# A bidirectional state-space scan: decay, step and mask in one array, both directions in one product

## What is computed

```
y[t] = sum over s <= t of exp(c_f[t] - c_f[s]) * (C[t].B[s]) * dt_f[s] * x[s]      forward
     + sum over s >= t of exp(c_b[t] - c_b[s]) * (C[t].B[s]) * dt_b[s] * x[s]      backward
     + what the carried states of other chunks add, for each direction
```

## Time and profile before

| | |
|---|---|
| median of three runs | 3008.32 us (2997.15 to 3011.02) |
| the profiled execution | 3002.91 us |
| its span in the trace | 3001.1 us |
| PE busy | 2875.6 us, 96% of the span |
| DVE, ACT, POOL busy | 846.9, 733.4, 245.7 us |
| granted PE clock, mean | 0.982 |

### The profile page before, as it was taken

How to read it: one execution, slowest core, us unless ns; L and a number is a source line. 1 busy time by engine, 2 the same in 40 slices (tenths; PEclk the granted TensorE clock), 3 DMA queues, 4 the chain that set the end, 5 groups by cost and what they waited for, 6 DMA issues and landing times.

```text
span 3001.1 us, 30849 instructions
## 1 busy us (share of the span) xinstructions
PE 2875.6 (96%) x12370; PEld 1831.9 (61%) x12370; DVE 846.9 (28%) x1568; ACT 733.4 (24%) x1712; POOL 245.7 (8%) x262
## 2 busy tenths in 40 slices
PE   7989998999997999999999999999999799999999
PEld 6768884555544666444444444445666577788888
DVE  1330005455463333200121000006555433202110
ACT  1330012554554333100011000004544422201100
POOL 3000001232331000000000000001212200000000
PEclk8999999999998999999999999999999999999999
DMA  9336765333331121122252442425334222357652
GB/s 230 85 103 174 196 195 144 101 98 96 93 100 42 51 56 50 56 74 76 75 175 81 122 126 77 126 74 149 101 99 110 64 71 71 83 151 214 177 152 87
DMA packets 530157, 330.40 MB, mean 110 GB/s; under 512 B 27504, under 2 KB 496864, under 8 KB 530016
## 3 DMA queue, kind: packets, MB, share of 16 engines
q1 hardware_dynamic: 519184, 296.36, 35.7%
q0 software_dynamic: 10528, 31.46, 4.3%
q10 hardware_dynamic: 304, 0.61, 0.1%
HBM read 327.05 MB, written 1.34 MB: 109 GB/s over the span
## 4 chain that ended last, share of the span: by engine, by line
PE 83%; ACT 7%; DVE 5%; issue 2%; PEld 1%; DMA 1%; DVEq 1%; POOL 0%; PEldq 0%; POOLq 0%; ACTq 0%; SPq 0%
PE ps L956 61%; PE ps L1388 4%; PE ps L1379 4%; PE ps L1370 3%; PE ps L1297 2%; ACT TMP L784 2%; DVE TMP L1841 2%; PE ps L1407 2%; PE ps L982 1%; PE ps L1428 1%; ACT TMP L790 1%; PE ps L966 1%; ACT BIG L796 1%; PEld ps L956 1%; DMA BIG<-bias_lines 1%
## 5 line engine op out<-in xcount | busy, mean ns | idle before, releaser
L956 PE MATMUL ps<-xnT,W 128*128 128x512 f32 (+2 forms) x4064 | 1326.5, 486 | 15.6 <-DVE TMP L1623 7.0
L956 PEld LDWEIGHTS ps<-xnT,W 128*128 128x128 f32 (+1 forms) x4064 | 772.1, 191 | 529.7 <-issue 449.9
L956 PE MATMUL ps<-BIG,W 128*128 128x256 f32 (+1 forms) x2528 | 773.3, 467 | 5.3 <-DVEq L402 2.7
L956 PEld LDWEIGHTS ps<-BIG,W 128*128 128x128 f32 x2528 | 481.1, 191 | 291.1 <-issue 245.9
L1841 DVE SCALAR_TENSOR_TENSOR TMP<-ps,prmT,TMP 128x510 f32<-128x510 f32 (+3 forms) x256 | 182.5, 714 | 141.1 <-ACT TMP L763 125.2
L597 ACT ACTIVATE xnT<-hT 128x512 f32<-128x512 f32 (+1 forms) x48 | 25.1, 523 | 568.0 <-DVE hT L1772 467.1
L574 ACT ACTIVATE TMP<-ps 128x512 f32<-128x512 f32 (+4 forms) x150 | 85.0, 572 | 233.1 <-PE ps L1388 94.3
L1772 DVE SCALAR_TENSOR_TENSOR hT<-ps,modc,hT 128x256 f32<-128x256 f32 x48 | 21.8, 481 | 374.2 <-PE ps L956 374.2
L555 POOL TENSOR_TENSOR BIG<-BIG,TMP 128x512 f32<-128x512 f32 x80 | 107.9, 1364 | 186.6 <-ACT BIG L796 186.6
L1388 PE MATMUL ps<-W,xnT 128*128 128x128 f32 x1024 | 122.6, 276 | 0.0
L2030 DVE TENSOR_TENSOR BIG<-TMP 128x512 f32<-128x512 f32 (+1 forms) x64 | 35.8, 559 | 303.1 <-ACT TMP L926 303.1
(11 more groups left out here) (273 smaller groups left out, 2134.5 us busy)
## 6 DMA issues: line engine op xcount, KB each, us to landing
W<-in_w_in SPq DMA_DIRECT2D x192, 512.0 KB, 4.0
W<-in_w_mlp SPq DMA_DIRECT2D x128, 512.0 KB, 4.1
W<-in_ada_w SPq DMA_DIRECT2D x96, 512.0 KB, 3.8
BIG<-cs_rows POOLq DMA_DIRECT2D x96, 256.0 KB, 4.8
W<-in_w_ssd_o SPq DMA_DIRECT2D x32, 512.0 KB, 4.0
W<-in_w_gate SPq DMA_DIRECT2D x22, 512.0 KB, 5.1
W<-in_w_up SPq DMA_DIRECT2D x22, 512.0 KB, 4.7
W<-in_w_down SPq DMA_DIRECT2D x16, 512.0 KB, 4.2
```

Of the source, the lines that this page charges most:

```text
L956: last = mm(dst, w[:, c, 0:m], rhs(k), start=k == 0, stop=k == total - 1)
```

## The change

The multiplication by the step dt moves from x to the masks, and the masks of the two directions are added before the product. `xc` holds plain x, once instead of twice, written by a copy. `masked` is now eight instructions of 128 columns, each `mt` times the step (a column of one number for each partition, out of `tabs`) times `cbm`, then a drain, then one addition of 512 columns that puts the sum into the first direction's buffer. `mready` counts chunks instead of directions. `outputs` has one term in place of two for the work inside the chunk. The other arrays keep their places in memory: a gap of 1024 columns is left where the second half of `xc` was.

```diff
@@ the arrays
-        (tabs, ssq, xs, xc, xcd, cbm, btm, mt, H, ysq) = carve(
-            TMP, (4, 4, 64), (T,), (4, T), (2, 4, S), (2, 2, S), (2, 4, P), (T,), (4, 4, P), (2, 3, S), (2, T))
+        (tabs, ssq, xs, xc, _, xcd, cbm, btm, mt, H, ysq) = carve(
+            TMP, (4, 4, 64), (T,), (4, T), (4, S), (D,), (2, 2, S), (2, 4, P), (T,), (4, 4, P), (2, 3, S), (2, T))
@@ PE, outputs
-                    R("mready", 2 * (n_ch * g + i) + 2)
+                    R("mready", n_ch * g + i + 1)
...
-                        for d in range(2):
-                            terms.append([(xc[:, d, ch, h * HD:(h + 1) * HD], mt[:, (2 * (n_ch * g + i) + d) % 4, h, :])
-                                          for h in (2 * pair, 2 * pair + 1)])
+                        terms.append([(xc[:, ch, h * HD:(h + 1) * HD], mt[:, (2 * (n_ch * g + i)) % 4, h, :])
+                                      for h in (2 * pair, 2 * pair + 1)])
@@ DVE, masked
                         c = 2 * (n_ch * g + i) + d
                         R("mexp", c + 1)
-                        V.tensor_tensor(mt[:, c % 4, :, :], mt[:, c % 4, :, :],
-                                        cbm[:, d, order[i], :].unsqueeze(1).to_broadcast([P, 4, P]), ALU.mult)\
-                            .then_inc(ssd[l, "mready"], 1)
+                        for h in range(4):
+                            V.scalar_tensor_tensor(out=mt[:, c % 4, h, :], in0=mt[:, c % 4, h, :],
+                                                   scalar=tabs[:, 0, order[i], span(g * 4 + 32 * d + h, 1)],
+                                                   in1=cbm[:, d, order[i], :], op0=ALU.mult, op1=ALU.mult)
+                    dve.drain()
+                    V.tensor_tensor(mt[:, (c - 1) % 4, :, :], mt[:, (c - 1) % 4, :, :], mt[:, c % 4, :, :], ALU.add)\
+                        .then_inc(ssd[l, "mready"], 1)
@@ DVE, xc
-                    for d in range(2):
-                        for b in range(n_ch // 2):
-                            last = V.tensor_tensor(
-                                xc[:, d, 2 * b:2 * b + 2, :].rearrange("p c (h e) -> p c h e", e=HD),
-                                PS[4 + b][:, :].rearrange("p (c h e) -> p c h e", c=2, e=HD),
-                                tabs[:, 0, 2 * b:2 * b + 2, span(g * 4 + 32 * d, 4)].unsqueeze(3)
-                                .to_broadcast([P, 2, 4, HD]), ALU.mult)
+                    for b in range(n_ch // 2):
+                        last = V.tensor_copy(flat(xc[:, 2 * b:2 * b + 2, :]), PS[4 + b][:, :])
```

## The result

The changed kernel takes 3026.86 us, the median of five runs (3023.43 to 3027.55), against 3008.31 us for five runs of the kernel before. The ratio is 1.007, with a 95% interval of 1.0048 to 1.0092: slower by 0.7%. In a later set of runs (experiment 11) the same pair gave 1.0076 (1.0062 to 1.0089). The forecast was +5 us on the profiled execution; its span went from 3001.1 to 3025.1 us, +24.

What follows compares the result with a forecast made beforehand. PE was taken as the bound, busy 96% of the span, except where outputs 1 in layer 0 wait for DVE. Terms 2.0 + 1.6 - 6.4 + 2.0 + 5.8 gave +5 us, on base 3006: 3011 us, range 2999 to 3029.

Steps and rivals of the forecast that it cites:

- The size of a masked: DVE, both scans: eight instructions, drain and addition take 2.93 us, 1.64 more than before (bounds 1.2 and 2.3 more).
- The stop: PE's wait ahead of outputs 1 in layer 0 grows from 1.79 to 3.9 us.
- A group of layer 0 without the clock: Layer 0, groups 0 to 6: masked 1 adds 1.64 us, outputs 1 to 3 lose 0.455 and 0.91; +0.28 a group.
- Layer 1: Layer 1, groups 0 to 6: outputs 0 and 1 lose 0.91 us a group, nothing takes it back; -6.4 us.
- The clock: Layer 0, PE's stop ahead of outputs 1: granted clock falls in half of seven groups, 1.65 us each; +5.8 us.
- The last groups: Last group of each layer, no fronts to cover the longer masks: +1.6 us in layer 0, +2.0 in layer 1.
- The slower one: Rival: layer 0's clock falls in every group and DVE steps do not overlap; +19 us, 3025 us, chance 0.18.

Runs made afterwards that it cites:

- experiment 11: The changed kernel itself, run again beside the kernel before on the same chip: 3022.16 us, ratio 1.0076.
- experiment 1: Changed kernel plus 14 overwritten PE products between outputs 0 and outputs 1, layer 0, groups 0 to 6: 3010.53 us, ratio 1.0029 to the kernel before.
- experiment 5: Changed kernel without the masks' addition, so PE multiplies two terms as before, with the eight masking instructions kept: 3024.69 us, ratio 1.0087 to the kernel before.

## Why the prediction was wrong

It said "no change" with 0.78 and gave "slower" 0.18. By its own steps:

- **The size of a masked, right where POOL is quiet.** A step of 0.26 us and 2.17 us for eight instructions were forecast from the earlier trace rows; 2.18 was measured. The stop was forecast at 3.9 us; it is 3.89 in six groups (2.49 in group 0, which started from 0.38). The rule of the Trainium skill (VectorE: DVE Perf Modes, The DRAIN you can't avoid), weighed there, would have given 2.8 us for the eight. The same section ends by saying that an operation which is not held starts earlier, and the prediction left that out; the trace agrees with the exception: each took 0.347 us at the median and the step was 0.26.
- **A group of layer 0 without the clock, right.** +0.28 forecast, +0.36 in experiment 1.
- **Layer 1, right in the main.** -0.91 a group forecast, -0.85 measured; over the six periods in the table -4.5 where the sum had -5.5, since two of them were 0.4 and 0.2 us longer.
- **The clock, wrong, and the largest miss.** The text had both facts: 1.79 us keeps the clock, 4.3 us loses it, and 3.9 is nearer the latter. It then counted "a fall in half of the seven groups", +5.8 us, because 3.9 was shorter than any stop with a row. The clock fell in all six groups with a stop of that length, for 2.0 us each: 12 us, 6 more than counted (and in all seven in experiment 11). The price of 1.65 us was too low as well, and it was a mean over 15 us in which PE was busy for only 7.3; the full cost is what the products behind the stop take more. Experiment 1 shows the cause by taking it away, experiment 5 that even 2.7 us would have been too long. The Trainium skill (TensorE: Matmul & The Clock Gate, Part 1), which has an idle array fall back to half its rate, was cited beside this step and agrees with the trace; it was given half its weight.
- **The last groups, undersized.** +1.6 and +2.0 us were forecast, +6.7 and +4.5 came (the table's 5.9 and 3.7 begin at front 2 of group 6 and so hold what the outputs of that group gained). Two steps failed. The first priced the products there as if their speed stayed as it was. In layer 0 outputs 1 and the states behind them took 4.0 us at 0.50 instead of 2.6 at 1.00, +1.4 where the sum had -0.5; in layer 1 the outputs took 5.40 us at 0.50 throughout, where before the clock was back at 0.91 in their second half (5.20), +0.2 where the sum had -1.3, and 0.5 us more came behind them. The second put POOL at nothing on DVE: of the +3.9 us up to outputs 1 in layer 0 (+2 forecast) 1.7 are masked 0 and `carried` beside POOL's multiplications. In layer 1 DVE's +3.8 is near the forecast 3.3. The prediction had named this collision only as something that might make masked 2 or 3 late in the middle groups, where it turned out to be covered.
- **The rivals.** The slower one had the right mechanism (the stop ahead of outputs 1 decides by its length) and tied it to steps on DVE that do not overlap. That condition was not needed: the point from which it decides lies near 2.5 us, not at 4.5. Its size, 3025, is right by luck in part: it had 6.6 us for the seven groups where 2.5 came, and 3.5 each for the last ones where 6.7 and 4.5 came.

A slip without effect: the row of outputs 2 and 3 is 64 MATMUL records, two for each of 32 products, and not 32 of them and 32 weight loads; it is 16 terms either way.

Summed by the prediction's own terms:

| term | forecast | from the two chains |
|---|---|---|
| layer 0, groups 0 to 6, without the clock | +2.0 | +2.5 |
| the clock in these groups | +5.8 | +12 |
| layer 0, last group | +1.6 | +6.7 |
| layer 1, groups 0 to 6 | -6.4 | -5.4 |
| layer 1, last group | +2.0 | +4.5 |
| sum | +5 | +20 |

The ratios 1.007 and 1.0076 of about 3002 us are 21 and 23; the rest of the profile's 24 us is the 2.7 that arose ahead of the scan and the 1.2 behind it.

## What to carry to other kernels

Work that leaves a busy engine is worth something only where that engine does not stand still, so look in each stage for the engine's next stop before counting what is saved; here the saving held in layer 1 and turned into a loss in layer 0, by the same edit. A stop of the matrix engine has a price beyond its length once it is long enough for the clock to fall, and if it recurs in each round of a loop, count the fall in each round. Before making a stop longer, see whether the work behind it can move to a place where its engine idles: one line moved was worth 7 us in the old kernel and, in layer 0 alone, some 28 us in the new one (1.0076 to 0.9984), while the same move in layer 1 as well took all of that back.

## What the runs showed of the hardware that was not expected

**DVE and POOL hold each other up, and with short DVE instructions it is DVE that pays.** With 512-column masks, POOL's multiplication took 1364 ns on the mean and the longest mask instruction 1757 (685 at the median); with eight 128-column ones POOL took 1283, while DVE's mean in the middle groups was 443 ns, and 345 with POOL's work cut down. In a list of L1876 alone, one of the 384 took as long as a whole POOL instruction (the columns are the shortest, median and longest duration):

```profile
L1876 DVE SCALAR_TENSOR_TENSOR TMP<-TMP x384: 336/347/1387, 542.2 to 2397.9; 128x128 f32<-128x128 f32 x192
```

Where POOL multiplied for 2.54 us, the eight took 2.03 us longer; where it did nothing, they took no longer. That the two engines take turns instruction by instruction fits this, but no run here tested it by itself.

**Groups settle at 58.0 us.** The periods of the changed kernel grow from 57.9 to 58.0 us and those of experiment 11 shrink from 58.3 to 58.05, with fronts 2 and 3 going from 13.73 to 13.89 us in the one and from 14.22 to 13.92 in the other. Experiment 5 (0.75 us less work on DVE and 0.44 more on PE in each of the four chunks) repeats at 58.0 us as well, there with fronts of 13.73 and a shorter fall. The clock's fall seems to move with the group until its cost is constant. What fixes this length stays open.
